# Mixer inverse: the second and third product of a level on half of the columns

## The reference, cut to what matters

```python
def step(S, inp):
    rt, wt, kt, vt, kkt, bt = inp
    sk = jnp.einsum('bhij,bhj->bhi', S, kkt)
    S = S * wt[:, :, None, :] - sk[..., None] * bt[:, :, None, :] + vt[..., None] * kt[:, :, None, :]
    return S, jnp.einsum('bhij,bhj->bhi', S, rt)

S, ys = lax.scan(step, S0, xs, reverse=reverse)
```

## Time and profile before

| engine | busy us | share of the span |
|---|---|---|
| TensorE, matmul | 3215.4 | 96% |
| TensorE, weight load (beside the matmuls) | 2855.2 | 85% |
| VectorE | 1992.5 | 60% |
| GpSimd | 875.7 | 26% |
| ScalarE | 535.4 | 16% |

### The profile page before, as it was taken

The page is one execution under the profiler, slowest core; times in us unless marked ns, Lnnn a source line. Parts: engine busy times, 40 slices in busy tenths (PEclk is TensorE's granted clock), DMA queues, the critical chain, the costliest instruction groups (busy, mean ns, idle before and its releaser), DMA issues.

```text
span 3342.3 us, 62917 instructions
## 1 busy us (share of the span) xinstructions
PE 3215.4 (96%) x27322; PEld 2855.2 (85%) x27322; DVE 1992.5 (60%) x3796; ACT 535.4 (16%) x1056; POOL 875.7 (26%) x710
## 2 busy tenths in 40 slices
PE   7999999699999899999999999999999999999999
PEld 4887454588888799999889999899899998998998
DVE  6886446566666376574747567464276575561673
ACT  2000010233433110110111011121010102120111
POOL 0000000122222177665036600000166200000564
PEclk9999999899999899999999999999999999999999
DMA  7465655100000145445334565334344442335353
GB/s 284 176 227 207 231 216 200 43 6 6 6 6 6 51 164 176 153 166 176 117 108 170 190 228 172 107 122 144 127 164 166 171 164 101 126 103 173 136 173 117
DMA packets 69793, 466.30 MB, mean 140 GB/s; under 512 B 7360, under 2 KB 10048, under 8 KB 16793
## 3 DMA queue, kind: packets, MB, share of 16 engines
q1 hardware_dynamic: 52272, 368.07, 31.8%
q0 software_dynamic: 12192, 87.04, 7.1%
q10 hardware_dynamic: 5065, 7.27, 0.7%
HBM read 456.59 MB, written 5.77 MB: 138 GB/s over the span
## 4 chain that ended last, share of the span: by engine, by line
PE 90%; DVE 7%; ACT 2%; issue 1%; DMA 0%; POOL 0%; DVEq 0%; ACTq 0%; POOLq 0%
PE ps L781 30%; PE ps L1222 14%; PE ps L675 13%; PE ps L836 8%; PE ps L852 4%; PE ps L1232 3%; PE ps L898 1%; PE ps L885 1%; PE ps L904 1%; PE ps L1251 1%; PE ps L1306 1%; PE ps L1281 1%; PE ps L1167 1%; PE ps L945 1%; PE ps L998 1%
## 5 line engine op out<-in xcount | busy, mean ns | idle before, releaser
L622 POOL TENSOR_TENSOR arena<-ring 128x512 f32<-128x512 f32 (+1 forms) x170 | 233.7, 1375 | 1458.5 <-DMA ring<-in_w_fx_gu 1013.9
L781 PE MATMUL ps<-arena 128*128 128x128 f32 x4400 | 521.7, 275 | 4.4 <-DVE arena L1760 2.6
L781 PEld LDWEIGHTS ps<-arena 128*128 128x128 f32 x4400 | 505.7, 192 | 6.3 <-DVE arena L1760 3.5
L781 PE MATMUL ps<-arena,ring 128*128 128x128 f32 x2200 | 275.3, 275 | 1.7 <-issue 1.7
L675 PE MATMUL ps<-arena,ring 128*128 128x256 f32 (+1 forms) x864 | 263.0, 466 | 0.0
L781 PEld LDWEIGHTS ps<-arena,ring 128*128 128x128 f32 x2200 | 261.0, 192 | 2.4 <-issue 1.8
L1746 DVE TENSOR_TENSOR arena<-ring 128x512 f32<-128x512 f32 (+1 forms) x170 | 202.4, 1195 | 93.4 <-DMA ring<-in_w_f_down 49.0
L628 POOL TENSOR_TENSOR arena<-ring,arena 128x512 f32<-128x512 f32 (+1 forms) x170 | 251.8, 1481 | 13.3
L675 PEld LDWEIGHTS ps<-arena,ring 128*128 128x128 f32 x864 | 164.2, 190 | 97.0 <-issue 83.7
L625 POOL TENSOR_TENSOR arena<-arena,ring 128x512 f32<-128x512 f32 (+1 forms) x170 | 219.7, 1292 | 13.3
L1771 DVE TENSOR_TENSOR arena<-arena,ps 128x256 f32<-128x256 f32 x130 | 54.7, 421 | 273.4 <-ACT arena L1404 271.9
(11 more groups left out here) (379 smaller groups left out, 5517.3 us busy)
## 6 DMA issues: line engine op xcount, KB each, us to landing
ring<-in_w_f_gu SPq DMA_DIRECT2D x88, 1024.0 KB, 5.0
arena<-in_ada_t POOLq DMA_DIRECT2D x72, 1024.0 KB, 5.4
ring<-in_w_fx_gu SPq DMA_DIRECT2D x44, 1024.0 KB, 4.9
ring<-in_w_f_down SPq DMA_DIRECT2D x36, 1024.0 KB, 4.9
ring<-in_w_fx_down SPq DMA_DIRECT2D x24, 1024.0 KB, 4.9
ring<-in_w_qk_a SPq DMA_DIRECT2D x18, 1024.0 KB, 5.2
ring<-in_w_qk_r SPq DMA_DIRECT2D x16, 1024.0 KB, 5.0
ring<-in_w_v_r SPq DMA_DIRECT2D x16, 1024.0 KB, 4.9
```

What stands on the lines that cost most here:

```text
L622: nc.gpsimd.tensor_tensor(both, quarter(s, 2, n), quarter(s, 3, n), ALU.add) \
L781: last = mm(out, weights[number][:, j * P:(j + 1) * P], inputs[number](base + j), start=(s.opens and j == 0 and number in (1, 5)), stop=(s ...
```

## The change: what it does

Level `lev` joins two neighbouring blocks of 2^lev columns. The product T x is non-zero, and changes `tri`, only in one of the two (the second block of each pair when q = 1, the first when q = 0); x^T `tri_t` only in the other. The changed kernel computes and subtracts those columns alone. The weights of each matmul stay the same, 64x64; the moving operand is now 32 of the 64 columns, in runs of 2^lev, and the 8 results lie side by side in 256 columns of the bank. The two VectorE subtractions read those 256 columns and update 256 of 512 elements of `tri` and of `tri_t`, in runs of 2^lev.

```diff
+        def columns(matrix, lev, second):
+            return matrix.rearrange("p (m s w) -> p m s w", s=2, w=2 ** lev)[:, :, second]
+
+        def packed(bank, lev, n, rows=slice(0, P)):
+            first, count = n
+            return ps[rows, bank, 32 * first:32 * (first + count)].rearrange("p (m w) -> p m w", w=2 ** lev)
...
-                            last = mm(ps[rows, 0, at(hd, c)], tri_t[rows, q, hd, c], x_sb[rows, hd, c],
-                                      start=True, stop=True)
+                            last = mm(packed(0, lev, (4 * hd + c, 1), rows), tri_t[rows, q, hd, c],
+                                      columns(x_sb[rows, hd, c], lev, q), start=True, stop=True)
...
-                            last = mm(ps[rows, 1, at(hd, c)], x_sb[rows, hd, c], tri_t[rows, q, hd, c],
-                                      start=True, stop=True)
+                            last = mm(packed(1, lev, (4 * hd + c, 1), rows), x_sb[rows, hd, c],
+                                      columns(tri_t[rows, q, hd, c], lev, 1 - q), start=True, stop=True)
...
             def level_done(u, lev):
                 q = u % 2
+                whole = lambda ap: ap.rearrange("p h c t -> p (h c t)")
                 v.wait_ge(*past(f"pe.t{u}_{lev}"))
-                tt(eight(tri[:, q]), eight(tri[:, q]), four_eight(0), ALU.subtract).then_inc(*step(f"dve.t{u}_{lev}"))
+                part = columns(whole(tri[:, q]), lev, q)
+                tt(part, part, packed(0, lev, (0, 8)), ALU.subtract).then_inc(*step(f"dve.t{u}_{lev}"))
                 v.wait_ge(*past(f"pe.tt{u}_{lev}"))
-                tt(eight(tri_t[:, q]), eight(tri_t[:, q]), four_eight(1), ALU.subtract).then_inc(*step(f"dve.tt{u}_{lev}"))
+                part = columns(whole(tri_t[:, q]), lev, 1 - q)
+                tt(part, part, packed(1, lev, (0, 8)), ALU.subtract).then_inc(*step(f"dve.tt{u}_{lev}"))
```

## The result

The changed kernel is slower: 3373.78 us median of 20 runs (3352.01 to 3393.68) against 3351.78 us (3343.5 to 3359.28), ratio 1.0059, 95% interval 1.0046 to 1.0072. The forecast was 3344 us. The runs also scatter 2.6 times as wide as before (41.7 us against 15.8).

A forecast was written before the change was run, and what follows sets the result against it. The prediction took TensorE to bound the kernel, busy 96% of the span. Pace 0, VectorE's waits 4.3 + 1.1 + 1.2 and tail 1 gave 7.6, say 8 us: median 3344 us, range 3332 to 3355.

The forecast's parts named there:

- Pace of the products: Level products on TensorE: weight loads set the instruction distance, so half the moving columns save 0 us.
- Rival A: Level products' pace falls: 22 us less at 19.4 ns, or 15 us by the skill's floor; 3328 us, chance 0.08.
- Tail: Last matmul of a product ends 27 ns sooner, so what follows L904 starts sooner: 1 us, at most 1.6.
- VectorE: The 120 level subtractions take 0.34 us instead of 0.60, saving 32 us of busy time.
- What reaches the end: VectorE's saving counts only where TensorE waits: 1.08 us a pair, 4.3 + 1.1 + 1.2 us in the mixer.
- C: Rival: short element runs in the level subtractions cost VectorE its gain, 0.60 us kept; 3351 us, chance 0.07.
- D: Rival: GpSimd's locks in the mixer take back VectorE's gain, 7 us in six places; 3351 us, chance 0.05.
- my forecast 0.73: Chance given to the main forecast for the whole kernel: about 8 us saved, 3344 us as a median.
- B: Rival: TensorE's clock falls more often in the mixer, two more per unit costing 37 us; 3381 us, chance 0.07.
- The evidence against B: From 1104 to 1112 us TensorE keeps clock 1.00 with 44 instructions and far more idle time.
- The base: The profiled execution, 3344.1 us, from which 8 us were taken; it lies 8 us below the median, 3351.8 us.

The follow-up runs named there:

- e8: The changed kernel unaltered, measured again beside the filled versions: 3372.87 us.
- e1: The changed kernel with both level products back on all 64 moving columns, short subtractions kept: 3343.55 us.
- e2: The changed kernel with an unread copy after each short subtraction, so VectorE takes its former time; products keep 32 columns: 3357.36 us.
- e5: The changed kernel with useless 128-column filler matmuls where TensorE waits, and one chunk step moved ahead of them: 3340.69 us.
- e7: The kernel before with the same useless 128-column filler matmuls where TensorE waits: 3342.41 us.

## Why the prediction was wrong, step by step

- **Pace of the products: 0 us. Right.** 0.93 us for 32 instructions before and after, and 2 moving columns go at about the pace of 128 (1.45 against 1.56 us for twelve). Rival A is dead. (Its two prices did not compare: 22 us counts the 72 products of the chain, 15 us all 120; for the 72 the second is 9 us.)
- **Tail: 1 us. The size was about right, by luck; the place was wrong.** The instructions of these products between 797 and 860 us, all at full clock (ns min/median/max), before and then changed:

```profile
L898 PE MATMUL ps<-arena,y x288: 218/218/267, 798.2 to 855.3; 64*64 64x64 f32 x144
L904 PE MATMUL ps<-y,arena x288: 218/218/219, 799.2 to 856.2; 64*64 64x64 f32 x144
L908 PE MATMUL ps<-arena,y x274: 218/219/241, 804.3 to 860.0; 64*64 64x32 f32 x137
L914 PE MATMUL ps<-y,arena x256: 218/219/220, 805.2 to 855.9; 64*64 64x32 f32 x128
```

  The last instruction of a product is as long with 32 columns as with 64, and where VectorE waits it starts 1.148 us behind the first start of L914 (median), exactly as behind L904. So the tail behind L904 gained nothing. What shrank is the head of the other product: the first two instructions of each L908 take 241 ns instead of 267, and L914 starts 0.03 us sooner. In the chain before, the piece was

```profile
816.35 1.08 PE ps L898 x32
```

  and the changed kernel has 1.05 us at 821.87. The Trainium skill (TensorEngine Tiling (Array Packing), Instruction Overhead), by which the tail would gain nothing, agrees with the last instructions (218 and 219 ns), not with the first two.
- **VectorE: 32 us of busy time, 0.34 us each. Right**: 32.1 us, 0.34 in the chain.
- **What reaches the end: 7 us. Nearly.** A pair of units at full clock takes 77.1 us (884.54 to 961.64), 1.0 less than before; forecast 1.1 and some of the tail. The idle places behind L2082 came out at 0.22 and 0.37 us. The one behind L2097 was mis-sized: 0.67 went to 0.44, not to 0.15, so it gave 0.23 instead of 0.50. The chain of the changed kernel shows why:

```profile
809.89 0.96 PE ps L914 x32
...
810.87 0.36 DVE arena L2110
...
811.27 0.66 PE ps L955 x4
```

  L2110 (L2097 of before) now starts when TensorE's own L914 ends, so shorter VectorE work can't bring it forward any more. The waits behind VectorE thus give 0.72 us a pair, and the ten shorter heads 0.28: together the 1.0. Rivals C and D did not come: a subtraction takes 418 ns at every level, and the pair at full clock kept its gain. At equal clock the whole change is worth 6 us, forecast 8.
- **The step that failed: "my forecast 0.73, B 0.07".** The sum was made at the clock of one profile: it put the clock at 0 us and left it to a rival, as a thing apart that might fall 5 times more. It was not apart. The change takes half of the moving columns out of two of the three level products (32 in each of 3840 instructions), and the clock followed. From 0.989 to 0.978 is 11 x 2.6 = 29 us, the term that was missing; less 6 that is 23, and 22 were measured. B's mechanism was right, and its place in part: two of the five falls stand behind the 1.56 us idle, three elsewhere. What I got wrong was its chance, 0.07, and the length and so the price of a fall. I priced one at 1.55 us, from the single short fall of the earlier trace rows. The pair with the fall at 867 us took 83.1 us instead of 77.1, so that one cost 6.0. Among the narrow products single falls lasted up to 20 us, and 27 us in e8, where those of before and e1 at the level products lasted 3 to 4 in their profiles. That the narrow work behind a fall keeps the clock down is my reading of this, not shown by a run of its own. Nor do the columns explain all: e2 has the same columns and lost 5 us, and what the shorter subtractions add to the falls stays open.
- **The evidence against B was read wrongly.** 1104 to 1112 us at clock 1.00 with little streaming was taken as proof of reserve. Right behind it, from 1112 to 1126 us, the same profile has a clock of 0.51, which I had seen and left aside. In the changed kernel that stretch at half speed starts at 1108 and lasts 41 us instead of 17, and the sum had no term for it.
- **The base.** The profiled execution of before (clock 0.992) was as good as the best of the 69 later ones (0.986 to 0.992). Its single fall among the level products made the clock look safe. The other two runs known by then, 3351.8 and 3355.62 us, were slower by 8 and 12 us; over the 69 runs time follows the clock, so most of that scatter was the clock's.

## What to carry to other kernels

Where weight loads set the pace, narrower moving operands save no TensorE time, and can cost its clock, as here. Before trimming columns from a stretch with TensorE waits in it, count the falls in several runs, not in one profile; a scatter of times that follows the mean clock is the sign. What did better here: halve the VectorE work and leave the matmuls whole (e1), or fill the waits with wide matmuls.

## What was not expected of the hardware

- 95 matmuls without use, in waits of 0.4 to 1.6 us, made a 3373 us kernel 32 us faster (e5), and the kernel before 10.5 us faster (e7).
- At 98% busy in both, TensorE was granted 1.00 with fillers of 128 moving columns and 0.92 with 2.
- The order of effects turned around: shortening 120 VectorE instructions by 0.26 us gains 8.5 us with full products (e1) and loses 16 with half ones (the changed kernel against e2). That is open.
